# Expert-choice layers: router on unnormalised rows, and the first gather split into one expert and three

## What is computed

```python
def moe_ec(h, router_w, w1, w3, w2):
    b, T, _ = h.shape
    cap = EC_CAPACITY * T // N_EXPERTS_2
    logits = jnp.einsum('btd,de->bte', h, router_w, preferred_element_type=jnp.float32)
    aff = jax.nn.softmax(logits, axis=-1)
    gate, idx = lax.top_k(jnp.swapaxes(aff, 1, 2), cap)
    bidx = jnp.arange(b)[:, None, None]
    xg = h[bidx, idx]
    a = jnp.einsum('becd,edf->becf', xg, w1)
    g = jnp.einsum('becd,edf->becf', xg, w3)
    y = jnp.einsum('becf,efd->becd', jax.nn.silu(a) * g, w2)
    y = y * gate[..., None].astype(y.dtype)
    return jnp.zeros_like(h).at[bidx, idx].add(y.astype(h.dtype))

x = x + g2l * moe_ec(rmsnorm(x, norm2_w[i]) * (1.0 + sc2l) + sh2l, ...)
```

## Time and profile before

| | us |
|---|---|
| median of three runs | 2209.57 |
| lowest, highest | 2205.31, 2211.0 |
| the profiled execution's own time | 2207.29 |
| its span, first to last instruction | 2205.5 |
| TensorE matmul busy | 2015.0 (91%) |
| TensorE weight load busy | 1058.8 (48%) |
| VectorE, ScalarE, POOL busy | 941.7, 648.6, 107.1 |

### The profile page before, as it was taken

The page is one execution under the profiler, slowest core; times in us unless marked ns, Lnnn a source line. Parts: engine busy times, 40 slices in busy tenths (PEclk is TensorE's granted clock), DMA queues, the critical chain, the costliest instruction groups (busy, mean ns, idle before and its releaser), DMA issues. The chain is left out here.

```text
span 2205.5 us, 24666 instructions
## 1 busy us (share of the span) xinstructions
PE 2015.0 (91%) x9986; PEld 1058.8 (48%) x9986; DVE 941.7 (43%) x1655; ACT 648.6 (29%) x1285; POOL 107.1 (5%) x121
## 2 busy tenths in 40 slices
PE   9987987989899999999899998988999899999887
PEld 6844443444387888878633333322445422222222
DVE  5776224444688878863622222121566311000002
ACT  5344023111277777662211111100235111111000
POOL 0101010000010110110100000000110000000000
PEclk9989999999899999999999999999999999999999
DMA  9537478899333433324489999999730599999997
GB/s 345 191 115 286 172 289 317 326 386 383 99 98 115 134 115 115 118 80 162 196 364 428 427 429 427 428 427 428 301 115 1 212 428 426 426 427 427 425 426 299
DMA packets 142768, 623.58 MB, mean 283 GB/s; under 512 B 10912, under 2 KB 61216, under 8 KB 104512
## 3 DMA queue, kind: packets, MB, share of 16 engines
q1 hardware_dynamic: 138144, 601.92, 68.4%
q0 software_dynamic: 2352, 16.91, 1.9%
q10 hardware_dynamic: 2160, 3.18, 0.4%
HBM read 620.80 MB, written 1.18 MB: 282 GB/s over the span
## 5 line engine op out<-in xcount | busy, mean ns | idle before, releaser
L2896 PE MATMUL bank<-slots,xgTe 128*64 128x512 f32 (+1 forms) x1664 | 373.4, 595 | 34.1 <-DMA slots<-in_moe_w 32.4
L3116 DVE TENSOR_TENSOR actse<-sge,bank 32x512 f32<-32x512 f32 (+1 forms) x48 | 32.8, 683 | 502.2 <-PE bank L2896 281.3
L2896 PEld LDWEIGHTS bank<-slots,xgTe 128*64 128x64 f32 (+1 forms) x1664 | 107.4, 124 | 276.2 <-issue 228.2
L2896 PE MATMUL bank<-slots,aTe 128*64 128x512 f32 (+1 forms) x704 | 163.4, 607 | 13.9 <-issue 13.9
L3014 ACT ACTIVATE sge<-bank 32x512 f32<-32x512 f32 (+1 forms) x48 | 28.4, 591 | 483.7 <-PE bank L2896 483.5
L527 PE MATMUL bank<-slots_r 128*128 128x512 f32 x416 | 163.9, 394 | 0.0
L526 PE MATMUL bank<-hT_r,slots_r 128*128 128x512 f32 x384 | 155.6, 405 | 0.0
L528 PE MATMUL bank<-slots_r 128*128 128x512 f32 x384 | 152.0, 396 | 0.0
L596 PE MATMUL bank<-slots,hT 128*128 128x512 f32 (+1 forms) x320 | 133.2, 578 | 4.5 <-DVE hT L493 3.0
L2123 DVE TENSOR_TENSOR slots_r<-slots,slots_r 128x2048 fp32r<-128x2048 f32 x32 | 76.7, 2398 | 68.3 <-ACT slots_r L2118 68.1
L372 POOL TENSOR_SCALAR rstd<-eps_rows 128x1 f32<-128x1 f32 (+5 forms) x41 | 17.8, 434 | 1772.4 <-ACT xn L443 621.2
(11 more groups left out here) (565 smaller groups left out, 3122.1 us busy)
## 6 DMA issues: line engine op xcount, KB each, us to landing
slots<-in_moe_w SPq DMA_DIRECT2D x148, 2048.0 KB, 28.6
slots<-in_ada_w SPq DMA_DIRECT2D x24, 2048.0 KB, 12.2
extra0e<-in_moe_w SPq DMA_DIRECT2D x23, 2048.0 KB, 27.3
slots<-in_ssd_in_w SPq DMA_DIRECT2D x48, 512.0 KB, 5.3
slots<-in_moe_w_gate SPq DMA_DIRECT2D x23, 1024.0 KB, 11.1
slots<-in_moe_w_up SPq DMA_DIRECT2D x23, 1024.0 KB, 13.6
slots<-in_moe_w_down SPq DMA_DIRECT2D x23, 1024.0 KB, 7.3
rowsB<-acum_rows POOLq DMA_DIRECT2D x16, 1024.0 KB, 5.8
```

The source lines that it names most:

```text
L2896: i = pe.matmul(bank[64 * n:64 * n + NJ * CAP, :], lhsT(4 * h + k), wv[:, 0, n * 512:(n + 1) * 512], start=(h == 0 and k == 0), stop=(h == ...
L3116: i = dve.tensor_tensor(acts[r_, :], sg[r_, :], psum[1][r_, :], ALU.mult)
```

## The change

The router works on the rows as they come, before the norm. TensorE transposes the raw rows tile by tile (`turn`, reading every fourth column), VectorE (for the last half tile ScalarE) copies them plainly to `hT`, and TensorE multiplies each tile with the router, into which VectorE has multiplied the gain (`score`). The shift's part of the logits becomes a product of its own, `bias`: the shift column, broadcast to 128x128, as weights and the router as 16 moving columns, 8 per stream. After the fold, VectorE applies root and bias with one instruction per tile. POOL's roots are now of the mean; ScalarE scales the rows into `xn`, half of the tiles before the exp and half behind it. The four filler matmuls at the start of the second stage are gone.

The first gather is for expert 0 alone, into two banks, one emptied by VectorE and one by ScalarE. `mark` is called for expert 0, for experts 1 to 3, and for the rest. The gather of experts 1 to 3 (`RESTS`, four banks in layer 0 and two in layer 1) stands on TensorE behind w1 of expert 0 and the transposes of the gates, ahead of the next group's quarter and w3; VectorE empties its banks after the second `weigh`, and TensorE waits for that before w1 of expert 1. Some semaphores are merged into one counter, `routed`, counted by the names in STEPS.

```diff
+        def root_of_mean(pool, at, n, width, done):
+
+            link = chain(pool, pool_step)
+            c = slice(at, at + n)
+            link(pool.tensor_scalar(rstd[:, c], eps_rows[:, c], 1.0 / width, EPS, ALU.mult, ALU.add))
+            pool.tensor_tensor(rstd[:, c], rstd[:, c], minus_half[:, 0:n], ALU.pow).then_inc(done, 1)
...
+                apart = lambda a: a.rearrange("p (h m j) -> p h m j", h=2, j=4)
+                shift = lambda j, k: modcol[:, l, 6 + k // 4, k % 4, sid[j]:sid[j] + 1]
+                turned_by = lambda i, h: ACTE if (i, h) == (T - 1, 1) else DVE
+                rest_full, rest_taken = sem("rest_full_" + tag), sem("rest_taken_" + tag)
+                STEPS = ("sub", "aff", "sv", "mark1", "mark2", "weigh1", "mark3", "weigh2")
+                routed = sem("routed_" + tag)
...
-                FIRST = [(n, UNITS[n:n + 4]) for n in range(0, len(UNITS), 4)]
+                FIRST = [(n, UNITS[n * len(UNITS) // 2:(n + 1) * len(UNITS) // 2]) for n in range(2)]
+                RESTS = [(n, UNITS[4 * n:4 * n + 4]) for n in range(len(UNITS) // 4)]
...
+                    def turn(i):
+
+                        for h in range(2):
+                            b = banks.open((tag, "xT", i, h), turned_by(i, h))
+                            pe.wait_ge(*b.emptied)
+                            for j in range(4):
+                                ins = pe.transpose(b.ap[:, j * P:(j + 1) * P], tiles_[i][:, 512 * h + j:512 * h + 509 + j:4], ident)
+                            ins.then_inc(bank_full, 1)
+
+                    def score(i):
+
+                        for h in range(2):
+                            b = banks[tag, "xT", i, h]
+                            pe.wait_ge(emptied[b.by], b.done)
+                        b = banks.open((tag, "quarters", i), DVE)
+                        pe.wait_ge(*b.emptied)
+                        for k in range(KD):
+                            rows_ = slice(32 * (k % 4), 32 * (k % 4) + 32)
+                            ins = pe.matmul(b.ap[rows_, 0:P], wide[:, k, :], hT[:, k, i * P:(i + 1) * P], start=(k < 4),
+                                            stop=(k >= 4), tile_position=(0, 32 * (k % 4)), skip_group_check=True)
+                        ins.then_inc(bank_full, 1)
+
+                    turn(0)
                     pe.wait_ge(wide_ready, 1)
-                    b = banks.open((tag, "quarters"), DVE)
+                    for i in range(1, T):
+                        turn(i)
+                        score(i - 1)
+                    score(T - 1)
+                    extra_room[2].freed = (bank_full, banks[tag, "quarters", T - 1].full)
+                    b = banks.open((tag, "bias"), DVE)
                     pe.wait_ge(*b.emptied)
-                    for k in range(KD):
-                        norm.wait_chunk(pe, k)
-                        rows_ = slice(32 * (k % 4), 32 * (k % 4) + 32)
-                        i = pe.matmul(b.ap[rows_, 0:T * P], wide[:, k, :], hT[:, k, 0:T * P], start=(k < 4), stop=(k >= 4),
-                                      tile_position=(0, 32 * (k % 4)), skip_group_check=True)
+                    for j in range(NJ):
+                        for k in range(KD):
+                            i = pe.matmul(b.ap[:, j * N_EXP:(j + 1) * N_EXP], shift(j, k).broadcast_to([P, P]), wr[:, k, :],
+                                          start=(k == 0), stop=(k == KD - 1))
                     i.then_inc(bank_full, 1)
...
                     b = banks.open((tag, "router"), DVE)
                     pe.wait_ge(*b.emptied)
                     for t in range(T):
-                        i = pe.matmul(b.ap[:, t * 16:(t + 1) * 16], quarters[:, t * P:(t + 1) * P], const("fold")[:, 0:16],
-                                      start=True, stop=True)
+                        pe.wait_ge(emptied[DVE], banks[tag, "quarters", t].done)
+                        i = pe.matmul(b.ap[:, t * 16:(t + 1) * 16], quarters[:, t * P:(t + 1) * P],
+                                      const("fold")[:, 16 * (t // NT):16 * (t // NT) + 16], start=True, stop=True)
...
-                    def fetch(bank, g, units):
+                    def fetch(bank, e0, n, units):
+                        w_ = n * CAP
                         for u, (k, j) in enumerate(units):
                             for t in range(NT):
-                                i = pe.matmul(bank[:, u * W:(u + 1) * W], xn[:, j * NT + t, k * P:(k + 1) * P],
-                                              onehot[:, t, j, g * W:(g + 1) * W], start=(t == 0), stop=(t == NT - 1))
+                                i = pe.matmul(bank[:, u * w_:(u + 1) * w_], xn[:, j * NT + t, k * P:(k + 1) * P],
+                                              onehot[:, t, j, e0 * CAP:(e0 + n) * CAP], start=(t == 0), stop=(t == NT - 1))
                         return i
 
-                    pe.wait_ge(onehot_ready, 1)
+                    pe.wait_ge(normed, norm.before + T)
+                    pe.wait_ge(*step("mark1"))
                     for n, units in FIRST:
-                        b = banks.open((tag, "xg", n), (DVE, ACTE)[n // 4 % 2])
+                        b = banks.open((tag, "xg", n), (DVE, ACTE)[n])
                         pe.wait_ge(*b.emptied)
-                        fetch(b.ap, 0, units).then_inc(bank_full, 1)
...
+                        if e == 1:
+                            pe.wait_ge(rest_taken, len(RESTS))
                         halves(psum[0], rows_of(e), 0, e, h1_full)
...
                         if e == 0:
+                            pe.wait_ge(*step("mark2"))
+                            for n, units in RESTS:
+                                settle(4 + n)
+                                fetch(psum[4 + n], 1, GROUP - 1, units).then_inc(rest_full, 1)
                             settle(2)
-                            pe.wait_ge(onehot_ready, 2)
+                            pe.wait_ge(*step("mark3"))
                         else:
                             pe.wait_ge(aT_ready, e)
                         if g + 1 < N_EXP // GROUP:
-                            fetch(psum[2], g + 1, UNITS[r * CHUNK:(r + 1) * CHUNK]).then_inc(fetched, 1)
+                            fetch(psum[2], GROUP * (g + 1), GROUP, UNITS[r * CHUNK:(r + 1) * CHUNK]).then_inc(fetched, 1)
...
-                    norm.pool(pool)
+                    for t in range(T):
+                        pool.wait_ge(squared, norm.before + t + 1)
+                        root_of_mean(pool, t, 1, D, rooted)
...
-                    norm.evacuate(act, ACTE)
-                    act.wait_ge(sub_ready, 1)
+                    b = banks[tag, "xT", T - 1, 1]
+                    act.wait_ge(bank_full, b.full)
+                    act.activation(hT[:, 4:8, (T - 1) * P:T * P], b.ap[:, :].rearrange("p (k n) -> p k n", n=P),
+                                   ACT.Copy).then_inc(emptied[ACTE], 1)
+
+                    def scale_rows(i):
+                        act.wait_ge(rooted, norm.before + i + 1)
+                        act.activation(xn[:, i, :].rearrange("p (h j m) -> p h m j", h=2, j=4), apart(tiles_[i]), ACT.Copy,
+                                       scale=rstd[:, i:i + 1]).then_inc(normed, 1)
+
+                    for i in range(T // 2):
+                        scale_rows(i)
+                    act.wait_ge(*step("sub"))
                     act.activation(lg[:, :, :], lg[:, :, :], ACT.Exp).then_inc(exp_ready, 1)
+                    for i in range(T // 2, T):
+                        scale_rows(i)
                     b = banks[tag, "g2"]
                     act.wait_ge(bank_full, b.full)
                     act.activation(g2[:, :], b.ap[:, :], ACT.Copy).then_inc(emptied[ACTE], 1)
...
-                    link(dve.memset(wide, 0.0))
-                    dve.tensor_copy(wide[:, :, 0:N_EXP], wr).then_inc(wide_ready, 1)
-                    norm.vector_scale(dve)
-                    norm.evacuate(dve, DVE)
-                    b = banks[tag, "quarters"]
-                    dve.wait_ge(bank_full, b.full)
-                    dve.tensor_copy(quarters, b.ap[:, 0:T * P]).then_inc(emptied[DVE], 1)
+                    if NJ == 1:
+                        link(dve.memset(wide, 0.0))
+                    for j in range(NJ):
+                        gains_ = ncol[:, l, 1, sid[j], :].unsqueeze(2).broadcast_to([P, KD, N_EXP])
+                        i = dve.tensor_tensor(wide[:, :, j * N_EXP:(j + 1) * N_EXP], wr, gains_, ALU.mult)
+                    i.then_inc(wide_ready, 1)
+                    dve.memset(ones, 1.0)
+
+                    def copy_quarters(i):
+                        copy_out(dve, DVE, (tag, "quarters", i), quarters[:, i * P:(i + 1) * P], P)
+
+                    for i in range(T):
+                        for h in range(2):
+                            b = banks[tag, "xT", i, h]
+                            if b.by == DVE:
+                                dve.wait_ge(bank_full, b.full)
```

(34 more changed lines are left out.)

46 lines of the change are left out of this document (19 added, 27 removed).

## The result

| | before | after |
|---|---|---|
| median of the runs taken side by side | 2208.74 (6 runs, 2203.87 to 2211.3) | 2218.84 (6 runs, 2217.84 to 2222.86) |
| the profiled execution's own time | 2207.29 | 2222.86 |
| its span | 2205.5 | 2220.7 |

The ratio is 1.0055, with a 95% interval of 1.0044 to 1.0066: the change makes the kernel slower by 10.1 us. The forecast was 2211.9 us, no difference, in a range that ended at 2218.5. The profiled execution is 4 us above its median, so its stages show a little more than the median does.

What follows compares the result with a forecast made beforehand. The prediction took the restart and pauses of the weight transfer stream to bound both expert stages. First stage +2.1, clock +1.4, second stage -1.15 made +2.35 us on 2209.57: 2211.9 us, range 2201.5 to 2218.5.

Steps and rivals of the forecast that it cites:

- What bounds the stages: Both expert stages: each ends a fixed time after its weight transfer stream restarts, plus every pause in it.
- F1: When weight slot one comes free in an expert stage: forecast 4.5 us earlier in the first, 3.2 in the second.
- F3 - F1: Slot one free to slot three free: 16.4 and 11.85 us; past 9.8 transfers pause, 6.6 and 2.05 us.
- Rival (b): Expert stages: the pause costs nothing, only the earlier first free slot counts; -7.7 us, 2201.9; chance 0.10.
- the stretch at zero: Sign in the profile: DMA share at zero for some 6 us in the first expert stage, 2 in the second.
- The gather: First gather, 32 moving columns: still 0.113 us a pass, 7.2 and 3.6 us; the second gather costs the same again.
- The clock: First stage's preparation on TensorE: lower granted clock costs zero to 2.8 us; the middle, 1.4 us, was taken.
- affinity transposes, from the stage's start: First stage, behind the router and g2: the new preparation lets these transposes come 2.6 us earlier.
- The second stage: Second expert stage: affinity transposes 3.0 us earlier, third piece at 1763.6 in place of 1764.74, so 1.15 us quicker.
- The sum: Whole kernel: +2.1 + 1.4 - 1.15 = +2.35 us on 2209.57, giving 2211.9 us, no difference.
- (a): Both gathers: the pace follows the moving columns, so together they cost today's 7.2 and 3.6 us; -9.9 us, 2199.7; chance 0.08.
- (c): Preparation in both stages: TensorE's short pieces run at 1.2 GHz for half that work; +8.45 us, 2218.0; chance 0.18.

Runs made afterwards that it cites:

- the late gather: The changed kernel with the gather of experts 1 to 3 moved behind w2 of expert 0, ahead of w1 of expert 1; 2218.13 us, ratio 1.0045.
- cheap_bias: The changed kernel with the old four-expert first gather and the bias computed with the router as 16-wide weights and two moving columns; 2198.57 us, ratio 0.9957.
- g2_late: cheap_bias with the output gate's group (g2) moved behind the affinity transposes, and three filler matmuls in place of six; 2200.16 us, ratio 0.9961.
- the split alone: The kernel before, with its old preparation, and of the change only the two gathers (expert 0, then experts 1 to 3); 2223.46 us, ratio 1.0071.

## Why the prediction was wrong, by its own steps

**What bounds the stages: right.** A stage ends a fixed time after its stream restarts, plus the pauses. The third piece came 11.2 us later and the first stage took 10.6 more; without the pause it took 7.0 less. Nine profiles of ten bear it out: counted from F1 + 9.8 us, or from F3 where that is later, the first stage's transfers run for 463.1 to 465.4 us until the DMA engines next stand still. The tenth is the late gather, whose pause lies behind that point.

**F3 - F1: right.** 16.32 and 11.82 us for 16.4 and 11.85. Rival (b), that the pause costs nothing, fell by the run without the second gather. One sign did not come as forecast: the stretch at zero was 3.9 us and not some 6, and 0.7 us and not 2, because a stream that starts anew is slow at first. The sum of 6.6 us held all the same, since that slow start is paid a second time.

**The gather: the step that failed.** "So narrowness buys nothing: I keep 0.113 us." The price of a pass is right at full clock (0.113 between the fillers, 0.114 with 96 columns). But narrowness is not free either: with 32 moving columns the granted clock went to 1.2 GHz although TensorE never paused, and the gather took 12.4 us, from its start to that of w1. I had bounded the pass from a row at full clock only, the fold's 16 columns, 8 passes and over in 1.06 us, too short a group to show what a long one does to the clock. The Trainium skill, "TensorE: Matmul & The Clock Gate", section "LDWEIGHTS (loading the stationary operand)", puts a load at its columns / 1.2, 107 ns for 128; the trace agrees with it at full clock, and not at the lower one: a pass took 0.193 us on average over the narrow gather, whose first 1.5 us were still at full clock.

**The clock: the wrong place.** "I take the middle, 1.4 us" was for the preparation's start alone, where the clock had fallen before. The clock did fall there, for 0.28 x 5 + 0.06 x 5 = 1.7 us of full-speed time (PEclk 0.72 and 0.94 in the first 10 us, before 0.60 and 0.72), but it cost nothing extra, and that was luck: the 32 transposes took 5.5 us from start to start for 3.5, and the four scores 2.9 us for 4.4 to 4.9, since a pass took 0.040 us (0.64 / 16) and not the 0.077 that I had carried over from another product. So the bias product began 8.44 us after the stage's start, where my sum gives 8.6. What was missing were two terms. In the first stage F1 was forecast 4.5 earlier and came 4.7 later, 9.2 us off:

| term, first stage | forecast | measured | off |
|---|---|---|---|
| affinity transposes, from the stage's start | 2.6 earlier | 0.3 later | 2.9 |
| start of the gather to start of w1 (9.0 before, 1.6 of it a wait) | 7.4 | 12.4 | 5.0 |
| start of w1 to F1 | as before, 3.69 | 5.07 | 1.4 |

The transposes' 2.9 us are the bias product, the fold and g2 at half clock: (4.82 - 3.6) + (1.87 - 1.06) + (3.73 - 2.46) = 3.3 us by their lengths, 3.1 from start to start, less the 0.2 us by which the bias product began sooner. cheap_bias gives them back: the transposes 3.2 us earlier than before. The 0.3 us of the smaller mark did come: the gather's start is 0.1 us earlier than before though the transposes are 0.3 later.

**The second stage: size off.** The third piece was to come 1.15 us earlier and came 1.0 later: the preparation gained 4.1 us where I had 3.0, the gather lost 0.5 and w1's first half 2.7 to the clock. That is 1.0 of the 3.1 us by which the stage is longer. Of the other 2.1, 1.7 come after the last weights have landed: from there to the end it takes 18.6 us, before 16.9, and the clock was at 1.2 GHz from 2198.6 to 2202.0 us, just ahead of that stretch. The change is hardly what made them: the kernels without the second gather and with g2 late show 18.6 us too, and the split alone, which has both narrow products of the gather, 16.9. Where they come from stays open.

**The sum.** Of the forecast's +2.35 us the clock term stood for 1.4. With the 9.2 that were missed in the first stage and 2.15 in the second in its place it would have been 0.95 + 9.2 + 2.15 = +12.3 us; the medians say +10.1, the profiled executions +15.6.

**Rivals.** (a) fell: the narrow passes cost what wide ones cost, at best. (c), the clock, was right in kind and near in its time, 2218.0 for 2218.84, but I had put it at the preparation, and most of it came at the gather; that its time fits is luck, since its 7.5 us were priced for another place. It had 0.18. I argued against it with "TensorE idles less than before", and idling was not what brought the clock down.

## What to carry to other kernels

On TensorE, count what a narrow product does to the clock of the work around it, not only what a pass costs: a long run of full weight loads with few moving columns (64 passes with 32 columns) ran at half clock, and the start of the next wide product with it, in all four profiles that have it without fillers. Turn such a product round if the narrow side can be the weights (0.59 in place of 4.82 us here), or keep it wide. In a stage paced by weight loads into reused slots, work added between the first uses of the slots costs its full length as soon as the margin to the stream (0.63 us here) is gone, and moving it to the next expert moved the pause and kept 5.3 of its 6.5 us.

## What the runs showed of the hardware that I had not expected

- The granted clock fell while TensorE was busy without a gap: in 64 passes of 128x128 fp32 weights with 32 moving columns it went to 1.2 GHz 1.5 us after the group began and stayed there for 13.7 us (12.3 and 11.6 us for the group with two different preparations), and in 32 passes with 16 moving columns after 2.5 us, for 6.8 us. All four profiles with 32 moving columns and no fillers show the same 13.7 us. With 128 moving columns the clock stayed at 2.4 GHz in four first-stage gathers of five (7.22 us before); in the fifth, cheap_bias, it dipped for 3.4 us. With eight 512-column matmuls mixed in it stayed up, in the one execution that was profiled.
- It also stayed low into the wide products behind: w1 took 8.47 in place of 7.09 us, and 9.78 us in the second stage.
- A low clock came with idle time as well: in 4.54 us of idling the clock fell, and the transposes and most of g2 behind it ran at half clock (g2_late, 3.64 in place of 2.46 us).
- A stream of transfers that starts anew is slow at first: 246 and 131 GB/s in its first two microseconds, 377 to 459 in the nine behind them.
- Whether the narrow columns alone do it, or only together with so many full weight loads, was not tried: no run had narrow columns with narrow weights for as long. Nor was it tried whether idle time has a part in the start of the fall: TensorE had stood idle for 1.04 and 0.95 us shortly before the narrow gather, and a run with filler there has the wide gather only.
